# Two layers of a hybrid block, one core: order of the last gate products of layer one and the first products of layer two

## The reference, cut to what matters

```python
for i in range(DEPTH):
    a = rms_norm(h, attn_norm[i])
    proj = a @ w_in[i]                      # q, k, v and the inputs of two more mixers
    ...
    h = h + mix @ w_out[i]
    f = rms_norm(h, ffn_norm[i])
    h = h + (silu(f @ w_ffn_gate[i]) * (f @ w_ffn_up[i])) @ w_ffn_down[i]
    h = h + sigmoid(h @ ple_w_gate[i]) * (p[i] @ ple_w_proj[i])
```

## Time and profile before

| | us |
|---|---|
| median of 3 runs | 1736.68 |
| lowest and highest run | 1735.91, 1738.02 |
| span of the profiled execution | 1734.4 |
| PE busy in it | 1689.0 (97%) |
| DVE busy | 1184.2 (68%) |
| ACT busy | 905.5 (52%) |

### The profile page before, as it was taken

How to read it: one execution, slowest core, us unless ns; L and a number is a source line. 1 busy time by engine, 2 the same in 40 slices (tenths; PEclk the granted TensorE clock), 3 DMA queues, 4 the chain that set the end, 5 groups by cost and what they waited for, 6 DMA issues and landing times.

```text
span 1734.4 us, 34119 instructions
## 1 busy us (share of the span) xinstructions
PE 1689.0 (97%) x14251; PEld 1463.6 (84%) x14251; DVE 1184.2 (68%) x1655; ACT 905.5 (52%) x1124; POOL 45.4 (3%) x51
## 2 busy tenths in 40 slices
PE   7999999998999999999999999999999989999998
PEld 5977799987987799988988888888888868899896
DVE  4888755537588765546566877778777684687875
ACT  5666433335576443334645545455454562465772
POOL 2000000000000000000000000000000000000130
PEclk9999999999999999999999999999999999999999
DMA  8666678554648757655222222223223123352122
GB/s 199 197 221 256 216 186 200 183 193 144 182 161 316 243 150 191 192 188 178 77 86 62 87 74 62 86 62 99 62 62 98 50 98 134 116 188 66 40 73 98
DMA packets 252857, 241.90 MB, mean 139 GB/s; under 512 B 32932, under 2 KB 212224, under 8 KB 252064
## 3 DMA queue, kind: packets, MB, share of 16 engines
q1 hardware_dynamic: 250896, 233.21, 43.4%
q0 software_dynamic: 1808, 6.50, 1.3%
HBM read 238.61 MB, written 1.08 MB: 138 GB/s over the span
## 4 chain that ended last, share of the span: by engine, by line
PE 84%; DVE 6%; ACT 3%; DMA 2%; DVEq 2%; issue 1%; ACTq 1%; SPq 1%; POOLq 0%
PE pg L2657 36%; PE pg L1318 36%; PE pm L1318 7%; PE pm L1321 2%; PE pm L2657 2%; DVE ring_r L576 1%; PE pm L2660 1%; DMA ring<-in_w_ffn_up 1%; DVE ring_r L1767 1%; ACT ring_r L569 1%; DVEq L1804 1%; DMA ring<-in_w_in 0%; DMA ring<-in_hg_w_out 0%; DMA cst<-in_cst 0%; SPq L2225 0%
## 5 line engine op out<-in xcount | busy, mean ns | idle before, releaser
L576 DVE TENSOR_TENSOR ring_r<-ring,ring_r 128x2048 fp32r<-128x2048 f32 (+1 forms) x126 | 284.3, 2261 | 168.4 <-ACT ring_r L569 162.4
L2657 PE MATMUL pg<-ring_r,work_r 128*128 128x512 f32 (+1 forms) x1632 | 376.9, 391 | 8.3 <-DVEq L3176 2.7
L2657 PEld LDWEIGHTS pg<-ring_r,work_r 128*128 128x128 f32 x1632 | 300.2, 190 | 76.6 <-issue 9.6
L1318 PE MATMUL pg<-ring_r,work_r 128*128 128x512 f32 (+3 forms) x1280 | 354.6, 383 | 4.2 <-DVEq L1768 2.1
L569 ACT ACTIVATE ring_r<-ring 128x2048 fp32r<-128x2048 f32 (+1 forms) x126 | 237.6, 1890 | 196.4 <-DMA ring<-in_w_ffn_up 79.2
L2657 PE MATMUL pg<-work_r,ring_r 128*128 128x256 f32 x2688 | 318.8, 281 | 0.5 <-DVE ring_r L576 0.5
L2657 PEld LDWEIGHTS pg<-work_r,ring_r 128*128 128x128 f32 x2688 | 317.3, 188 | 2.0 <-DVE ring_r L576 1.1
L1318 PE MATMUL pg<-ring_r 128*128 128x512 f32 (+3 forms) x752 | 284.2, 378 | 1.1 <-DVEq L831 1.1
L1318 PEld LDWEIGHTS pg<-ring_r,work_r 128*128 128x128 f32 x1280 | 235.4, 188 | 48.6 <-DVEq L1768 4.1
L1318 PE MATMUL pg<-work_r,ring_r 128*128 128x512 f32 (+1 forms) x976 | 264.0, 360 | 1.0 <-POOLq L943 1.0
L1318 PEld LDWEIGHTS pg<-work_r,ring_r 128*128 128x128 f32 x976 | 173.0, 189 | 27.9 <-POOLq L943 1.5
(11 more groups left out here) (402 smaller groups left out, 1798.5 us busy)
## 6 DMA issues: line engine op xcount, KB each, us to landing
ring<-in_w_in SPq DMA_DIRECT2D x36, 1024.0 KB, 5.3
ring<-in_hg_w_in SPq DMA_DIRECT2D x48, 512.0 KB, 4.0
ring<-in_w_ffn_gate SPq DMA_DIRECT2D x44, 512.0 KB, 4.1
ring<-in_w_ffn_up SPq DMA_DIRECT2D x44, 512.0 KB, 5.4
ring<-in_w_ffn_down SPq DMA_DIRECT2D x22, 1024.0 KB, 4.9
ring<-in_ada_w SPq DMA_DIRECT2D x16, 1024.0 KB, 9.3
ring<-in_hg_w_in SPq DMA_DIRECT2D x64, 256.0 KB, 3.0
ring<-in_w_out SPq DMA_DIRECT2D x12, 1024.0 KB, 5.9
```

The costliest lines, as they stand in the source:

```text
L576: W.low_done(V.tensor_tensor(lo, W.raw(i, name)[:, 0:lo.shape[1]], W.hi(i, name).bitcast(f32), ALU.subtract))
L1318: return T.matmul(out_, lhsT, rhs, start=first, stop=last)
L2657: return T.matmul(out_, lhsT, rhs, start=first, stop=last)
```

## The change

In the first of the two layers the gate products run in another order, (0,0,0), (0,0,1), (1,0,0), (0,1,0), (1,0,1), (0,1,1), (1,1,0), (1,1,1), written by `ple_gates_by_tile`. The transposes of the next layer's tile 0 move into the middle of (1,1,1). Sigmoids, additions and squares follow the new order; those of the second half of tile 1 move into layer two. For layer two, the transposes of tile 1 move behind dak (0,0), and dak (0,1) comes directly behind them, ahead of daq (1,0). `pp` and `psig` of layer one move to `mixT`, the junk of its squares to `xn`. The last layer keeps its order. Nothing is computed more or less often.

```diff
+        pp_of = lambda i: mixT[:, 0:2048] if i + 1 < DEPTH else mix[:, 0:2048]
+        psig_of = lambda i: mixT[:, 2048:3072] if i + 1 < DEPTH else mix[:, 2048:3072]
...
 @block.scalar, sigmoid_tile(j, n, t):
+                name, k = f"pleg{n}", 2 * t + n if j + 1 < DEPTH else 2 * n + t
+                if k == 2:
+                    e_pused.wait(act, j, 1)
+                if k == 3:
+                    e_h.wait(act, j, 5)
...
 @block.scalar, start of layer i:
                 norm0_high(p_attn, A_IN[0], 0, 0)
                 if i:
+                    norm0_high(p_attn, A_IN[0], 0, 1)
+                    split_high(act, i, "daq_1")
+                    e_pused.wait(act, i - 1, 2)
+                    squares(1, 0, slice(0, 512))
+                    sigmoid_tile(i - 1, 1, 1)
+                    split_high(act, i, "dak_0")
                     e_h.wait(act, i - 1, 6)
-                    squares(1, 1, slice(512, D), junk_ple)
+                    squares(1, 1, slice(512, D))
+                    e_rows.set(act.drain())
+                    split_high(act, i, "dak_1")
...
                 e_rows.wait(act, i, 3)
                 e_xn.set(A.activation(xn3[:, 1, :], h3[:, 1, :], ACT.Copy, scale=rstd[:, 1:2]))
-                split_high(act, i, "dak_0")
+                if i == 0:
+                    split_high(act, i, "dak_0")
                 norm0_high(p_attn, A_IN[0], 1, 0)
                 norm0_high(p_attn, A_IN[0], 1, 1)
...
-                    if k + 3 < len(w_in_pieces):
+                    if k + 3 < len(w_in_pieces) and not (i and k == 0):
...
 @block.scalar, end of layer i:
+                sigmoid_tile(i, 0, 0)
...
-                    for t in range(NT):
-                        e_pused.wait(act, i, t + 1)
-                        squares(t, 0, slice(0, 512), junk_ple)
+                    e_pused.wait(act, i, 1)
+                    squares(0, 0, slice(0, 512))
+                    sigmoid_tile(i, 1, 0)
+                    e_h.wait(act, i, 5)
+                    squares(0, 1, slice(512, D))
+                    e_rows.set(act.drain())
                     split_high(act, i + 1, "daq_0")
-                    sigmoid_tile(1, 0)
-                    split_high(act, i + 1, "daq_1")
-                    e_h.wait(act, i, 5)
-                    squares(0, 1, slice(512, D), junk_ple)
-                    e_rows.set(act.drain())
-                    sigmoid_tile(1, 1)
+                    sigmoid_tile(i, 0, 1)
...
 @block.tensor, queries_and_keys:
                     GEMM.wait_free(pe, "dak", i)
                     tile_by_columns("dak", 0, 0)
+                    if i:
+                        tile_transposes("norm0_t1", i, xn3, e_xn, 1, 1)
+                        tile_by_columns("dak", 0, 1)
                     e_aT.wait(pe, i, 3)
                     W.used(tile_by_columns("daq", 1, 0), "daq_0")
...
+                def ple_gates_by_tile():
+                    for n, t, f in ((0, 0, 0), (0, 0, 1), (1, 0, 0), (0, 1, 0), (1, 0, 1), (0, 1, 1), (1, 1, 0), (1, 1, 1)):
+                        name = f"pleg{n}"
+                        wt = weights(f"{name}_{f}", 4, 512)
+                        if t == f == 0:
+                            GEMM.wait_free(pe, name, i)
+                        e_aT.wait(pe, i, 8 + 2 * t + f + 1)
+                        for c in range(4 * f, 4 * f + 4):
+                            last = triple(...)
+                            if n == t == 0 and c == 3:
+                                tile_transposes("hT_t1", i, h3, e_h, 3, 1)
+                            if n == t == 1 and c == 5:
+                                tile_transposes("norm0_t0", i + 1, xn3, e_xn, 1, 0)
+                        if t and f:
+                            GEMM.done(last)
+                        elif t:
+                            W.used(last, f"{name}_0")
+                        elif f:
+                            e_pleg.set(last)
...
 @block.vector, start of layer i:
                 norm0_low(p_attn, A_IN, 0, 0)
+                if i:
+                    norm0_low(p_attn, A_IN, 0, 1)
+                    low("daq_1")
+                    e_psig.wait(dve, i - 1, 4)
+                    V.tensor_scalar(n_c[:, 1:2], ss[:, 1:2], 1.0 / D, EPS, ALU.mult, ALU.add)
+                    e_h.set(add_gated(i - 1, psig_half(i - 1, 3), 1, slice(512, D), 4))
+                    low("dak_0")
+                    tile_root(i, 1)
+                    e_rows.set(dve.drain())
...
                 norm0_low(p_attn, A_IN, 1, 0)
                 norm0_low(p_attn, A_IN, 1, 1)
                 low("dak_1")
...
 @block.vector, end of layer i:
-                e_pused.set(add_gated(psig_half(0), 0, slice(0, 512), 1))
+                e_pused.set(add_gated(i, psig_half(i, 0), 0, slice(0, 512), 1))
...
                 if i + 1 < DEPTH:
+                    e_psig.wait(dve, i, 2)
+                    V.tensor_scalar(n_c[:, 0:1], ss[:, 0:1], 1.0 / D, EPS, ALU.mult, ALU.add)
+                    e_h.set(add_gated(i, psig_half(i, 1), 0, slice(512, D), 2))
+                    first_rows(i + 1)
                     split_low(dve, i + 1, "daq_0")
-                    e_psig.wait(dve, i, 3)
-                    V.tensor_scalar(n_c[:, 0:NT], ss[:, 0:2], 1.0 / D, EPS, ALU.mult, ALU.add)
-                    e_h.set(add_gated(psig_half(2), 0, slice(512, D), 3))
-                    first_rows(i + 1)
-                    e_h.set(add_gated(psig_half(3), 1, slice(512, D), 4))
+                    e_pused.set(add_gated(i, psig_half(i, 2), 1, slice(0, 512), 3))
```

More of the change, by code:

```diff
@@ L2343, in _, with sigmoid_tile @@
             split_high(act, 0, "daq_0")
+            def sigmoid_tile(j, n, t):
+                name, k = f"pleg{n}", 2 * t + n if j + 1 < DEPTH else 2 * n + t
[3 more added lines that the diff above has]
+                    e_h.wait(act, j, 5)
+                if t == 0:
+                    e_pleg.wait(act, j, n + 1)
+                else:
+                    GEMM.wait_filled(act, name, j)
+                last = A.activation(psig_half(j, k), GEMM.buf(name)[:, t * 512:(t + 1) * 512], ACT.Sigmoid)
+                if t:
+                    GEMM.release(last, name)
+                e_psig.set(act.drain())
             for i in range(DEPTH):
@@ L2622, in _ @@
                     e_pleg.wait(act, i, 2)
-                    A.activation(psig_half(2), gates[:, 0:512], ACT.Sigmoid)
+                    A.activation(psig_half(i, 2), gates[:, 0:512], ACT.Sigmoid)
                     e_psig.set(act.drain())
@@ L2636, in _ @@
                             GEMM.wait_filled(act, "pleg1", i)
-                        last = A.activation(q3(psig_half(3), NT)[:, t, :], gates[:, last_gates(1, t)], ACT.Sigmoid)
+                        last = A.activation(q3(psig_half(i, 3), NT)[:, t, :], gates[:, last_gates(1, t)], ACT.Sigmoid)
                         if t:
@@ L2660, in tr, with tile_transposes @@
                     return T.transpose(out_, in_, ident)
-                def tile_transposes(name, src, event, at, t):
-                    event.wait(pe, i, at + t)
-                    M.wait_free(pe, name, i)
+                def tile_transposes(name, j, src, event, at, t):
+                    event.wait(pe, j, at + t)
+                    M.wait_free(pe, name, j)
                     for c in range(KC):
@@ L2717, in queries_and_keys @@
                 def queries_and_keys():
-                    tile_transposes("norm0_t0", xn3, e_xn, 1, 0)
+                    if i == 0:
+                        tile_transposes("norm0_t0", i, xn3, e_xn, 1, 0)
                     GEMM.wait_free(pe, "daq", i)
@@ L2731, in queries_and_keys @@
                     W.used(tile_by_columns("dak", 1, 0), "dak_0")
-                    tile_by_columns("dak", 0, 1)
+                    if i == 0:
+                        tile_by_columns("dak", 0, 1)
                     GEMM.done(tile_by_columns("dak", 1, 1))
@@ L2753, in ple_gate @@
                     GEMM.done(last)
+                def ple_gates_by_tile():
[6 more added lines that the diff above has]
+                        for c in range(4 * f, 4 * f + 4):
+                            last = triple(GEMM.buf(name)[:, t * 512:(t + 1) * 512], part(A_PLE, every, c, slice(t * P, (t + 1) * P)),
+                                          part(wt, every, c % 4), c == 0, c == KC - 1)
+                            if n == t == 0 and c == 3:
[8 more added lines that the diff above has]
+                            e_pleg.set(last)
                 def ple_gate_columns(k):
@@ L3149, in first_rows, with add_gated @@
                 e_xn.set(V.tensor_scalar(xn3[:, 0, :], h3[:, 0, :], rstd[:, 0:1], None, ALU.mult))
+            def add_gated(j, half, rows_, cs, turn):
+                e_psig.wait(dve, j, turn)
+                V.tensor_tensor(half, half, q3(pp_of(j), NT)[:, rows_, cs], ALU.mult)
+                dve.drain()
+                return V.tensor_tensor(h3[:, rows_, cs], h3[:, rows_, cs], half, ALU.add)
```

(7 more changed lines are left out.)

33 lines of the change are left out of this document (13 added, 20 removed).

## The result

| | before | changed |
|---|---|---|
| median of 5 runs, us | 1736.16 | 1750.25 |
| lowest and highest | 1735.44, 1738.02 | 1747.77, 1750.62 |
| span of the profiled execution, us | 1734.4 | 1747.2 |

The ratio is 1.0077, 95% interval 1.0066 to 1.0088: slower by 14.1 us by the medians. The profiled execution took 1749.29, 2.1 above its span. 12.8 us separate the two spans. The kernel before was run again beside each set of experiments: its medians there are 1736.76 us (15 runs, beside the first four experiments), 1735.88 (27 runs, beside the next four) and 1737.2 (15 runs, beside the last).

What follows compares the result with a forecast made beforehand. TensorE, busy 97% of the span, was taken as the bound. Waits and a clock fall of 18.2 us, less 5.8 before, gave 12.4; xbc0 11.9 later made 1736.68 + 11.9 = 1748.6 us, range 1744.0 to 1751.5.

Steps and rivals of the forecast that it cites:

- step 1: Gates of layer one: PE waits 3.2 us ahead of (1,0,0) for pleg1_0's low part from DVE.
- step 4: Start of layer two: PE waits 1.8 us ahead of daq (0,0), where 2.63 was; the clock was expected to hold.
- step 5: Layer two: PE waits 1.3 us ahead of daq (0,1) for daq_1's low part, 1.0 ahead of dak (0,0) for dak_0's.
- step 7: Behind tile 1's transposes: PE waits 6.5 us ahead of dak (0,1), as dak_1's low part stands behind tile 1's.
- Step 8: At dak (0,1): the clock falls in the long wait, costing 1.8 to 2.7 us more; 2.7 taken.
- step 9: Ahead of xbc0: xbc0_0's load waits for daq_0's slot, so 1.5 us of a formerly hidden load come out.
- the rival that the clock falls twice: Clock also falls in the 3.2 us wait, or later in the short waits: +1.8 us, 1750.4; chance 8%.
- 5.8 us, all that a better order can bring: Layers' border before the change: idle times of 0.91, 2.63 and 0.5 us plus 1.8 for slow daq (0,0).
- the change does what it says: Rival: PE is fed without a stop, border idle time and clock fall go: up to 5.8 us less, 1730.9; chance 5%.
- Step 3: Norm of tile 0: rows ready at 418.8, PE at its transposes at 419.9, so the 0.91 us wait is gone.
- Tables on ACT: Sigmoids between copies and squares on ACT: no table switch expected at returns to the sigmoid, nothing put into the sum.

Runs made afterwards that it cites:

- the filled waits: Changed kernel plus matmuls nobody reads, 10 ahead of (1,0,0) and 24 ahead of dak (0,1): 1745.89 us, ratio 1.0057.
- the best version: Changed kernel with third and fourth gate groups swapped, pleg1_0's and dak_1's low parts moved earlier, tile 0's transposes at the end of (1,1,0): 1736.15 us, ratio 0.9994.
- a fourth: Changed kernel with dak (0,1) moved back behind dak (1,0), DVE's order kept: 1741.28 us, ratio 1.0027.

## Why the prediction was right, and where it wasn't

Forecast 1748.6, range 1744.0 to 1751.5; measured 1750.25. Sign, place and cause were right, and the largest term was read from the order on DVE's list. Point by point, forecast and first trace after:

| step of the prediction | forecast, us | measured, us |
|---|---|---|
| 1, wait ahead of (1,0,0) | 3.2 | 2.96 |
| 4, ahead of daq (0,0) | 1.8 | 1.25 |
| 5, ahead of daq (0,1) and dak (0,0) | 1.3, 1.0 | 1.38, 0.62 |
| 7, ahead of dak (0,1) | 6.5 | 6.09 |
| 8, the clock behind that wait | 2.7 | 2.4 |
| 9, xbc0_0's load | 1.5 | 1.15 |
| a fall in the first wait | 0, a rival with 8% | 1.4 |
| stretch or span, longer by | 11.9 | 12.7 |

*Steps 1 and 7* are shown: each wait was taken away alone, by moving its low part, and the gain was the wait with its fall (5.0 and 8.3 us of the stretch). For step 7, moving the product instead of the low part gave 7.3, since 2.4 us of wait were left.

*How the terms add up.* The forecast counts a wait from 2.80 us behind a group's start; the trace lists it from the end of the row, which is 0.2 later (3.02 to 3.04). Counted as in the forecast, step 1 is 3.2 as forecast, step 4 is 1.5, step 5 1.6 and 0.8, step 7 6.4 and step 9 1.35. So steps 4, 7, 9 and the second wait of 5 were forecast 0.1 to 0.3 too long, and daq (0,1) 0.3 too short. One reason is in DVE's rows: I gave daq_0's low part 2.4 us, but the next instruction starts 2.20 behind it (418.56, 420.76). That the stretch came within 0.8 us of the forecast is in part luck: the fall that I left out (1.4) is partly made up by waits (0.4) and a clock term (0.3) taken too large.

*Step 8 and the rival that the clock falls twice.* The place and the level of the second fall were right. The first fall is where the reasoning was weakest. I set 3.2 us between an idle time of 1.37 without a fall and 4.6 with one, and gave the fall 8%. It came in three of four traces, and the rival's own 1750.4 is the better forecast of the median. Nothing in the rows stood for 8%: between two rows so far apart, even odds would have been honest. Of the sizes (1.8 to 2.7 for a fall) the second held, the first didn't: 2.4 and 1.4, measured apart by the filled waits. The 1.8 was too large already for the row that it came from, which ends at a stop: 4.58 is to be held against 3.03, not against 2.80. The other row, the kernel's first 12 in 5.46 us, has the pace of the low level, but the column of the granted clock reads 1.00 there.

*"5.8 us, all that a better order can bring"* was added up wrongly. The fall in it is 4.58 - 3.03 = 1.55, not 1.8, and it is no loss of its own: with the 2.6 us gap filled it was gone and the time stayed, since daq_1's low part was due at the same time anyway. The step that failed is that I priced a slow group without asking what is late next; I had the row (0.49, released by L576) and took it for a wait of its own. Taking away the fall alone is worth nothing. Whether it comes back in full when low parts are also sooner, as the rival "the change does what it says" supposes, no run shows.

*Step 3* held: the 0.91 us ahead of the transposes are gone, since the normed rows were ready at 418.6 and PE came at 419.8 (in the trace without the first fall, too, no wait stands ahead of them). *Tables on ACT* held too: one load of 1.28 us at 402.42, and none ahead of the sigmoid at 425.95 that follows squares and a high part. The Trainium skill ("ScalarE: Activation LUTs", Rules for kernel authors) says to do all functions of one table set before switching; in this trace the returns to the sigmoid behind squares and copies brought no switch.

*Why no version came out clearly ahead.* Unbroken, the stretch would take about 47.2 us, an estimate from rows: 16 groups at 2.80 and three times eight transposes at 0.8. The kernel before loses 6.4 us against that, the changed one 19.1, the best version 5.2. In the best, waits of 0.79, 0.65, 0.60 and 1.12 stand where 0.91, 2.63, 0.49 and a fall of 1.55 stood, and most stops also lengthen the row ahead of them by 0.2. So 1.2 us are left as gain, too little for the medians. What stays open is the cause of those waits: DVE has 8.3 us of work between the normed rows and daq (0,1), which fits its timeline, but shortening it wasn't tried.

## What to carry to other kernels

Before moving a product forward on an engine that works in order, list every operand it needs with the place of its producer on the other engine's list; a counted semaphore makes the product wait for all that is written ahead of that operand, here even for what the product behind it was to cover. When an order is changed on one engine, the lists of the others must be changed with it: one line on DVE was worth 8 us here, and the new order itself nothing measurable. And taking away a slow or idle stretch on the busiest engine is a gain only if the next operand is ready sooner; look at the first wait behind it.

## What was not expected of the hardware

The granted clock fell to the 1.2 GHz level in a wait of 2.96 us with full work ahead of it in three traces and not in a fourth, where the wait cost 1.4 us less. The fourth is of a program that differs from the others only behind that wait, so it looks like a difference between executions; both traces of the changed kernel itself show the fall, and no program has shown both cases in a trace. The six runs of the fourth lie at 1740.6 to 1740.8 us and at 1741.8 and more, which fits a fall in some of them, but isn't shown. Behind the 6.1 us wait 60 matmuls took 16.36 to 16.77 us in four traces, against 14.2 without a fall: 2.1 to 2.6 us a fall. In that wait the clock was still at 1.00 from 436 to 440 and fell less than 2 us before work came back.
